# A hybrid diffusion trunk layer: 28 of the 32 input blocks in groups of 512 channels, latents moving over stationary weights, weights moving over stationary context tokens

## Reference

```python
proj = h @ lp['w_in']                    # 2048 x 9216, h = modulated RMSNorm of x
xr, gr, q, k, v, gates = jnp.split(proj, SPLITS, axis=-1)   # 1024,1024,1024,1024,1024,4096 wide
# modulation: m = silu(c) @ w_mod + b_mod   (2048 x 12288), split in six rows of 2048
```

## Time and profile before

| | us |
|---|---|
| median of 3 runs | 2874.71 (2873.83 to 2875.45) |
| profiled execution, its own time | 2875.51 |
| span of its instructions | 2873.9 |
| TensorE matmuls busy | 2801.5 (97% of the span) |
| VectorE busy | 2107.7 (73%) |
| ScalarE busy | 1498.9 (52%) |
| HBM traffic | 263 GB/s over the span |

### The profile page before, as it was taken

One profiled execution on the slowest core, in us unless ns is written; L12 is line 12 of the kernel. 1 busy time (PEld: TensorE's weight loads), 2 busy tenths in 40 slices (PEclk: granted clock), 3 DMA queues, 4 the chain that ended last, 5 costly groups with the idle time before them and its releaser, 6 DMA issues.

```text
span 2873.9 us, 42975 instructions
## 1 busy us (share of the span) xinstructions
PE 2801.5 (97%) x15938; PEld 2466.8 (86%) x15938; DVE 2107.7 (73%) x1918; ACT 1498.9 (52%) x1480; POOL 293.3 (10%) x358
## 2 busy tenths in 40 slices
PE   7999999999999999999999996999999999999998
PEld 5589999999999999999998775888888888888886
DVE  2339677696777777773344577888888888888898
ACT  4411121114555555552233445777777777777776
POOL 1000000002111111100000001000010110110110
PEclk9999999999999999999999997999999999999999
DMA  9877686774333333374434666999999999999997
GB/s 369 306 268 252 201 273 214 224 256 130 121 112 117 114 113 115 117 218 127 123 134 132 248 235 249 358 402 396 394 395 395 396 394 396 393 391 385 390 394 297
DMA packets 301767, 757.51 MB, mean 264 GB/s; under 512 B 20584, under 2 KB 184976, under 8 KB 237344
## 3 DMA queue, kind: packets, MB, share of 16 engines
q1 hardware_dynamic: 277280, 650.01, 61.8%
q0 software_dynamic: 23456, 100.72, 10.8%
q10 hardware_dynamic: 928, 5.33, 0.5%
HBM read 700.61 MB, written 55.37 MB: 263 GB/s over the span
## 4 chain that ended last, share of the span: by engine, by line
PE 91%; DVE 4%; DMA 2%; ACT 2%; issue 2%; SPq 0%; DVEq 0%; ACTq 0%; POOL 0%; POOLq 0%
PE ps L533 16%; PE ps L535 16%; PE ps L534 16%; PE ps L2357 10%; PE ps L2359 10%; PE ps L2358 10%; PE ps L2487 3%; PE ps L2489 3%; PE ps L2488 3%; PE ps L2214 2%; PE ps L2425 1%; DMA raw<-in_w_mod 1%; DVE rsd L1782 1%; PE ps L2237 1%; PE ps L2226 1%
## 5 line engine op out<-in xcount | busy, mean ns | idle before, releaser
L458 DVE TENSOR_TENSOR we_lo<-raw,we_hi 128x2048 fp32r<-128x2048 f32 x384 | 877.2, 2289 | 113.3 <-ACT we_hi L453 113.2
L453 ACT ACTIVATE we_hi<-raw 128x2048 fp32r<-128x2048 f32 x384 | 736.6, 1919 | 260.6 <-PE ps L535 260.6
L2357 PE MATMUL ps<-hi,w_lo 128*128 128x320 f32 x2048 | 645.0, 315 | 10.9 <-DVE w_lo L412 10.9
L2358 PE MATMUL ps<-lo,w_hi 128*128 128x320 f32 x2048 | 635.2, 310 | 0.0
L2359 PE MATMUL ps<-hi,w_hi 128*128 128x320 f32 x2048 | 634.9, 310 | 0.0
L412 DVE TENSOR_TENSOR w_lo<-raw,w_hi 128x2048 fp32r<-128x2048 f32 x115 | 263.4, 2291 | 226.3 <-ACT w_hi L402 224.2
L2357 PEld LDWEIGHTS ps<-hi,w_lo 128*128 128x128 f32 x2048 | 386.7, 189 | 22.2 <-issue 20.7
L533 PE MATMUL ps<-we_hi,xs_lo 128*128 128x512 f32 x1024 | 399.5, 390 | 0.1
L535 PE MATMUL ps<-we_hi,xs_hi 128*128 128x512 f32 x1024 | 399.0, 390 | 0.0
L534 PE MATMUL ps<-we_lo,xs_hi 128*128 128x512 f32 x1024 | 398.9, 390 | 0.0
L2358 PEld LDWEIGHTS ps<-lo,w_hi 128*128 128x128 f32 x2048 | 387.1, 189 | 0.0
(11 more groups left out here) (433 smaller groups left out, 3828.8 us busy)
## 6 DMA issues: line engine op xcount, KB each, us to landing
raw<-in_w_e_gate SPq DMA_DIRECT2D x128, 1024.0 KB, 7.4
raw<-in_w_e_up SPq DMA_DIRECT2D x128, 1024.0 KB, 7.4
raw<-in_w_e_down SPq DMA_DIRECT2D x128, 1024.0 KB, 11.4
raw<-in_w_in SPq DMA_DIRECT2D x144, 512.0 KB, 6.2
mod_raw<-in_w_mod SPq DMA_DIRECT2D x64, 1024.0 KB, 5.5
raw<-in_w_mod SPq DMA_DIRECT2D x64, 512.0 KB, 7.7
raw<-in_w_o SPq DMA_DIRECT2D x64, 512.0 KB, 4.9
d_proj<-stage POOLq DMA_DIRECT2D x32, 320.0 KB, 6.3
```

The lines of the kernel that those rows point to most:

```text
L453: act.activation(we_hi[:, k % NEH, :], raw_slot(k), ACT.Copy).then_inc(hi_ready, 2)
L458: TTn(we_lo[:, k % NEH, :], raw_slot(k), we_hi[:, k % NEH, :].bitcast(F32), ALU.subtract).then_inc(lo_ready, 2)
L2357: pe.matmul(out, wl, hi[:, k, ms], start=(k % 16 == 0), stop=False)
L2358: pe.matmul(out, wh, lo[:, k, ms], start=False, stop=False)
```

## The change

Of the 32 blocks, 28 are taken as `WIDE` = 7 groups of 4 blocks (512 channels). A group is 4 units of 4 k tiles x 512 channels, loaded with `wide` (2 KB rows). In a unit, TensorE does for each of the 4 blocks 4 k tiles x 3 matmuls with weights stationary and the 512 latents moving, into banks 0 to 3, and then 4 k tiles x 3 with the 128 context tokens stationary and 512 weight columns moving, into bank 4: 60 matmuls a unit. The sums run over the four units of a group. The context product comes out with tokens on the partitions, so ScalarE copies it to `ctx_rows`, TensorE turns it (4 transposes, in the next group after block 1 of its first unit), and ScalarE copies the result to the last 128 columns of `stage4`. GpSimd stores a group in one DMA of 1280 KB. `stage4` lies over part of the old `stage`, which the last four blocks (u = 28 to 31) still use, in the old way; so their first copy waits until all 7 stores have landed (`stage_free`, value `WIDE`). `sum_mod` writes to bank 7 for the first three rows, and still comes after every eighth unit. VectorE's order is the same. TensorE's loop is gone: every unit is written out. GpSimd loads head 0's `xr` and recurrent weights after group 6, not after block 26.

```diff
-            for u in range(32):
-                wait(pool, "in_taken", 2 * (u + 1))
-                pool.dma_start(d_proj[u * P:(u + 1) * P, :], stage[:, u % 2, :]).then_inc(S["in_stored"], 16)
...
+            for g in range(WIDE):
+                wait(pool, "in_taken", 5 * (g + 1))
+                pool.dma_start(d_proj[4 * g * P:(4 * g + 4) * P, :].rearrange("(b p) n -> p b n", p=P), stage4[:]
+                               ).then_inc(S["in_stored"], 16)
+                stored("in_stored", (g + 1) * 16, "stage_free")
+                if g % 2:
+                    r = g // 2
+                    if r:
+                        pool.wait_ge(S["m_stored"], r * 32)
+                    load_bias(r, m_row2)
+                    wait(pool, "m_row_ready", r + 3)
+                    store_modulation(r, m_row2)
+            pool.wait_ge(S["zero_stored"], TT * 16)
+            load_recurrent(0)
...
-            for u in range(32):
+            def context_rows(g):
+
+                act.wait_ge(halves_used, used((Q_IN + g + 1) * 4))
+                act.activation(ctx_rows[:], ps[:, 4, :], ACT.Copy).then_inc(S["ctx_rows"], 1)
+
+            def context_columns(g):
+
+                act.wait_ge(S["ctx_turned"], g + 1)
+                act.activation(stage4[:, :, N_LAT:N_TOK], blocks(ps[:, 4, :]), ACT.Copy).then_inc(S["in_taken"], 1)
+
+            for u in range(4 * WIDE):
+                g, kq = u // 4, u % 4
+                if kq == 0 and g:
+                    context_rows(g - 1)
+                split_hi(act, Q_IN + g, kq + 1)
+                if kq == 0 and g:
+                    context_columns(g - 1)
+                if kq == 3:
...
+                        wait(act, "stage_free", g)
+                    for b in range(4):
+                        act.wait_ge(S["in_a_done"], 4 * g + b + 1)
+                        act.activation(stage4[:, b, 0:N_LAT], ps[:, b, :], ACT.Copy).then_inc(S["in_taken"], 1)
+            for u in range(4 * WIDE, 32):
+                if u == 4 * WIDE:
+                    context_rows(WIDE - 1)
                 split_hi(act, Q_IN + u // 4, u % 4 + 1)
+                if u == 4 * WIDE:
+                    context_columns(WIDE - 1)
                 if u == 31:
                     gates_hi(0)
                 act.wait_ge(S["in_a_done"], u + 1)
-                wait(act, "stage_free", u - 1)
+                wait(act, "stage_free", WIDE + max(0, u - 1 - 4 * WIDE))
...
-            with pe.Fori(0, 4) as g:
-                for n in range(8):
-                    unit_wait(pe, Q_IN + g * 2 + n // 4, n % 4)
-                    for half in range(2):
-                        wait(pe, "in_taken", (g * 8 + n) * 2 + half - 1)
-                        last = unit_piece(n % 4, half, range(KT), 5 + half)
-                        last.then_inc(*((S["in_a_done"], 1) if half == 0 else (halves_used, 2)))
-                sum_mod(g)
+            def turn_context(g):
+
+                pe.wait_ge(S["ctx_rows"], g + 1)
+                for b in range(4):
+                    last = turn(ps[:, 4, b * P:(b + 1) * P], ctx_rows[:, b * P:(b + 1) * P])
+                last.then_inc(S["ctx_turned"], 1)
+
+            def wide_unit(g, kq):
+
+                unit_wait(pe, Q_IN + g, kq)
+                ks = range(4 * kq, 4 * kq + 4)
+                for b in range(4):
+                    if kq == 0:
+                        wait(pe, "in_taken", 5 * (g - 1) + b + 1) if g else wait(pe, "bank_taken", TT + b + 1)
+                    for k in ks:
+                        s = slice(k % 4 * 512 + b * P, k % 4 * 512 + (b + 1) * P)
+                        last = three(pe, ps[:, b, :], w_hi[:, kq % 2, s], w_lo[:, kq % 2, s], hi[:, k, 0:N_LAT],
+                                     lo[:, k, 0:N_LAT], k == 0, k == KT - 1)
+                    if kq == 3:
+                        last.then_inc(S["in_a_done"], 1)
+                    if kq == 0 and b == 1 and g:
+                        turn_context(g - 1)
+                if kq == 0:
+                    wait(pe, "in_taken", 5 * g) if g else wait(pe, "bank_taken", 2 * TT)
+                for k in ks:
+                    s = slice(k % 4 * 512, (k % 4 + 1) * 512)
+                    last = three(pe, ps[:, 4, :], hi[:, k, N_LAT:], lo[:, k, N_LAT:], w_hi[:, kq % 2, s], w_lo[:, kq % 2, s],
+                                 k == 0, k == KT - 1)
+                last.then_inc(halves_used, 2)
+
+            for g in range(WIDE):
+                for kq in range(4):
+                    wide_unit(g, kq)
+                if g % 2:
+                    sum_mod(g // 2)
+            for u in range(4 * WIDE, 32):
+                unit_wait(pe, Q_IN + u // 4, u % 4)
+                for half in range(2):
+                    if u > 4 * WIDE:
+                        wait(pe, "in_taken", N_TAKEN + 2 * (u - 4 * WIDE) + half - 1)
+                    last = unit_piece(u % 4, half, range(KT), 5 + half)
+                    last.then_inc(*((S["in_a_done"], 1) if half == 0 else (halves_used, 2)))
+                    if u == 4 * WIDE and half == 0:
+                        turn_context(WIDE - 1)
+            sum_mod(3)
```

More of the change, by code:

```diff
@@ L63 @@
 MOD_TILES = (2, 2, 3, 2, 2, 3, 2, 0)
+WIDE = 7
+N_TAKEN = 5 * WIDE
 MOD_FROM = [sum(MOD_TILES[:n]) for n in range(8)]
@@ L187, in trunk @@
         assert s0 + 15360 + 2 * UB <= PLACED["rows1"] and mod_at + NMOD * UB + 192 <= s_end
+        stage4 = at("stage4", [P, 4, N_TOK], F32, s0 + 2048)
+        ctx_rows = at("ctx_rows", [P, 512], F32, s0 + 2048 + 4 * N_TOK * 4)
+        assert 2048 + 4 * N_TOK * 4 + 2048 <= 15360
         v_stage = at("v_stage", [P, TT, 512], F32, s0)
@@ L323, in trunk @@
             "sqrt_x", "xn_ready", "x_turned", "xt_act", "xt_dve", "b_loaded", "m_row_ready", "m_stored",
-            "zero_stored", "row_act", "start_used", "cols_taken", "mod_used", "mod_summed", "rows3_turned", "a1_ready", "tok_hi", "tok_lo",
+            "zero_stored", "row_act", "start_used", "cols_taken", "mod_used", "mod_summed", "ctx_rows", "ctx_turned", "rows3_turned", "a1_ready", "tok_hi", "tok_lo",
             "bank_done", "bank_taken", "v_stored", "in_a_done", "in_taken", "in_stored",
@@ L387, in half_of, with sum_bank @@
             return slice(p * 1024, (p + 1) * 1024)
+        def sum_bank(g):
+            return 7 if g < 3 else 0
         def gate_slot(j):
@@ L601, in mod_tiles @@
                                  ).then_inc(mod_loaded[k % NMOD], 16)
-            for j in range(4):
-                load(Q_IN, j, tall(w_in2, j, j * P))
+            for kq in range(4):
+                load(Q_IN, kq, wide(w_in, kq, kq, 0))
             for u in range(32):
@@ L610, in _ @@
                     sp.dma_start(C["rope"][:], a["rope"]).then_inc(S["rope_loaded"], 16)
-                    sp.wait_ge(S["in_stored"], 25 * 16)
+                    sp.wait_ge(S["in_stored"], WIDE * 16)
                     for turned, n in (("k_turn", 24), ("q_turn", 16)):
@@ L617, in _ @@
                 c0 = (u + 4) * P if u < 28 else GATE_COL + (u - 28) * P
-                if u < 28:
+                if u // 4 + 1 < WIDE:
+                    load(Q_IN + u // 4 + 1, u % 4, wide(w_in, u % 4, u % 4, (u // 4 + 1) * 512))
+                elif u < 28:
                     load(Q_IN + u // 4 + 1, u % 4, tall(w_in2, u % 4, c0))
@@ L812, in store_modulation @@
                                    ).then_inc(S["m_stored"], 16)
-            for u in range(32):
-                wait(pool, "in_taken", 2 * (u + 1))
+            for g in range(WIDE):
[13 more added lines that the diff above has]
+            for u in range(4 * WIDE, 32):
+                n = u - 4 * WIDE + 1
+                wait(pool, "in_taken", N_TAKEN + 2 * n)
                 pool.dma_start(d_proj[u * P:(u + 1) * P, :], stage[:, u % 2, :]).then_inc(S["in_stored"], 16)
@@ L820, in _ @@
                     load_rows(0, "k", 24, "k_loaded")
[L821 to L824, removed]
+                stored("in_stored", (WIDE + n) * 16, "stage_free")
                 if u == 30:
@@ L827, in _ @@
                     load_bias(3, m_row3)
[L828 to L834, removed]
             pool.sem_inc(phase, 1)
@@ L1069, in gates_hi @@
                 act.activation(lw_hi[:], C["lru_w"][:], ACT.Copy).then_inc(S["row_act"], 1)
-            for u in range(32):
+            def context_rows(g):
[12 more added lines that the diff above has]
+                if kq == 3:
+                    if g == 0:
+                        act.wait_ge(S["v_stored"], 4 * 16)
+                    else:
+                        wait(act, "stage_free", g)
[5 more added lines that the diff above has]
+                    context_rows(WIDE - 1)
                 split_hi(act, Q_IN + u // 4, u % 4 + 1)
+                if u == 4 * WIDE:
+                    context_columns(WIDE - 1)
                 if u == 31:
@@ L1580, in mod_row2 @@
                 m = (m_row3 if g == 3 else m_row2)[:]
```

(7 more changed lines are left out.)

## The result

| | before | after |
|---|---|---|
| median, us | 2874.95 (4 runs, 2873.83 to 2875.45) | 2849.05 (4 runs, 2847.91 to 2849.62) |
| profiled execution, own time | 2875.51 | 2848.87 |
| its span | 2873.9 | 2847.3 |
| forecast, median | | 2850.0 (2844 to 2862) |

The ratio is 0.991, with a 95% interval of 0.9895 to 0.9926: 25.9 us faster, clear of no change; 24.7 were forecast.

A forecast was written before the change was run, and what follows sets the result against it. TensorE's time was taken to bound the block stage. Matmuls -13.4, transposes +3.1, loop -16.9 and hand-over +2.5 summed to -24.7 us, so a median of 2850.0 us, range 2844 to 2862.

The forecast's parts named there:

- The step: Groups' 512-column matmuls: 226.7 ns between starts, columns at 2.4 GHz plus 13.3 ns, gaining 13.4 us.
- Rival C: In the groups, 512-column matmuls with stationary weights run slower; at +20 ns a step 2883.6 us; chance 0.03.
- rival D: Each matmul costs only 2.5 ns beyond its columns, so the matmuls gain 2.5 us, time 2861; chance 0.02.
- The transposes: Four added per group on TensorE, 0.11 us each, none hidden: 3.1 us added.
- The loop: TensorE's three taken branches at row sums, and the half clock behind them, go: 16.9 us gained.
- Rival B: Fetching the written-out code holds TensorE at the edges as the branch did: 16.9 us back, 2866.9; chance 0.05.
- The hand-over: From groups to last four blocks, TensorE waits at block 29 on the store: 1.8 us stall plus 0.7 clock.
- Rival A: The last group's big store lands late, and the bias too: 2871.5 us in full, 2856 at median landing; chance 0.13.
- VectorE: At group edges, 85% full and not the bound; may wait 1 us for the later bias, hidden from TensorE.
- the cover: VectorE's work stays ahead of TensorE if the bias arrives by 25.8 us into the next group; 19 us expected.
- Sum: Whole kernel: the terms add to -24.7 us, giving 2850.8 us for the profiled execution and 2850.0 for the median.
- the stages behind: Heads and later stages, full of matmuls, start when this stage ends and pass its gain on unchanged.

The follow-up runs named there:

- e3: The changed kernel with each of the seven groups' four transposes done three times over; 2858.85 us, ratio 0.9952.
- e1: The kernel before, with TensorE's four groups of eight blocks written out instead of looped, nothing else changed; 2857.59 us, ratio 0.9942.
- e5: The changed kernel with each group's 1280 KB store issued twice, both landed before buffer release and bias loads; 2861.57 us, ratio 0.9954.
- e6: The changed kernel with six groups of four blocks instead of seven, and eight blocks in the old way; 2857.16 us, ratio 0.9941.

## Why the prediction was right

*The step.* 226.7 ns, as taken from the value stage; the arrangement doesn't matter. Rival C (a slower step) and rival D (2.5 ns on top of the columns, the rule of the Trainium skill, TensorE: Matmul & The Clock Gate, section "Wait — 56ns, not 53.3ns?") are refuted by the timeline: at 215.8 ns the six steps would take 1.29 us and they take 1.36. The gain of 13.4 us stands.

*The transposes.* 3.1 us forecast; 7 x 0.50 = 3.5 measured, e3 has 0.106 for each further one.

*The loop.* 16.9 us forecast, 16.2 by e1's median and 16.6 by the traces: from the first row sum to the fourth are 360.63 us before and 344.06 in e1. Rival B is refuted by e1 too.

*The hand-over.* 1.8 us of stall and 0.7 of clock forecast. The store landed in 6.3 us for 7, the gap is 1.17 where 0.15 is usual, so 1.0 us, and the clock stayed at 1.00. Rival A didn't happen here, but it is real: e5 and e6 show it at 9.6 and 5.9 us with half clock behind.

*VectorE.* Here one term was mis-sized, without effect. Landing times of the seven stores, us, min/median/max, and VectorE's row of the first edge:

```profile
DMA to landing us min/median/max: 5.9/9.4/11.7
```

```profile
328.39 0.69 DVE L1626 TENSOR_TENSOR m_row<-ps,m_row 128x512 f32<-128x512 f32 x1 [3.49 <-DMA m_row<-in_b_mod]
```

The wait for the bias is 3.5 us, where at most 1 was forecast, because I took 7 us for the odd groups' stores as well. They took 11.7, 11.1 and 10.1 us, the first of them beside two tiles of `w_mod` and a unit of weights; the even ones took 5.9, 8.5, 9.4 and 6.3. The bias came 22.3 us after the next group's first matmul (328.39 less 306.05) for the 19 forecast, and the cover, up to 25.8 us, held.

*Sum.* With what was measured of each term, -13.4 + 3.5 - 16.6 + 1.0 = -25.5. The stage itself, from its first matmul to the fourth row sum, is 668.85 - 195.49 = 473.36 us before and 642.78 - 194.80 = 447.98 after, 25.4 less:

```profile
195.49 0.30 PE L2357 MATMUL ps<-hi,w_lo 128*128 128x320 f32 x1
...
668.85 1.92 PE L2369 MATMUL ps<-mod_acc,pick_row 128*32 128x512 f32 x16
```

```profile
194.80 0.39 PE L542 MATMUL ps<-hi,w_lo 128*128 128x512 f32 x1
...
642.78 1.92 PE L2414 MATMUL ps<-mod_acc,pick_row 128*32 128x512 f32 x16
```

The profiled executions are 26.6 us apart, the medians 25.9. The rest of the 26.6 is no term of the prediction: the stage began 0.7 us earlier, and head 0's wait for `k` has 0.6 (between starts 1.57 before, 0.99 after). So each mechanism was right, but part of the closeness is luck: the hand-over was put 1.5 us too dear, the transposes 0.4 and the loop's gain 0.3 the other way. And as forecast the stages behind are unchanged: from head 0's first transpose to the end of the span 2873.9 - 677.5 = 2196.4 us before, 2847.3 - 650.86 = 2196.4 after.

## What to carry to other kernels

Cost a matmul by the distance between starts, and write that distance as columns at the granted clock plus a constant: the constant is what fewer, wider matmuls save. Where an engine stops at each end of a loop and the named releaser finished long before or serves the next unit, look at the branch itself; a body half as long does as well as none. When a new buffer lies over an old one, the hand-over costs whatever the last store before it takes beyond its cover (1.0, 5.7 and 9.5 us in the change, e6 and e5); ask first which slot is free anyway.

## What was not expected of the hardware

A taken branch of TensorE took 5.0 us in a body of 1536 matmuls and weight loads and 3.9 in one of 3072, both behind a row sum, and 0.23 in one of 768 between blocks. And two stores of the same 1280 KB took 5.9 and 11.7 us by their place in the stage. The latter stands behind a row sum: SP's queue had waited 13.9 us there for VectorE, and then issued two tiles of `w_mod` and a unit of weights within 5 us.
